# Output projections tile by tile, eight row buffers in the combine, and a rebuilt group norm, in a two-layer encoder with mixture of experts

## The chip, the cores and the metric

One Trainium2 chip; the kernel runs on one of its cores. Its engines work side by side and meet only through semaphores: TensorE (PE) multiplies matrices, VectorE (DVE) and ScalarE (ACT) compute elementwise, GpSimd (POOL) builds masks and issues gathers, SyncE (SP) issues weight loads. The metric is the device time of one execution in microseconds, lower is better.

## The reference

Two batches of 256 tokens of width 1024 (512 token rows in all) go through two layers. Layer 0 mixes with a gated recurrence and a delta-rule recurrence (RWKV-7), layer 1 with windowed attention; behind each stands a mixture of 32 experts, two of them for a token.

```python
def trunk(x):
    for i in range(2):
        h = rms_norm(x, norm_mix[i])
        mix = recurrent_mixer(h, ...) if i == 0 else window_attention(h, ...)
        x = x + mix
        h = rms_norm(x, norm_ffn[i])
        x = x + hier_moe(h, ...)

# end of recurrent_mixer, its last steps: per-head group norm (8 heads of 64), bonus, gate, output projection
y = y_f + y_b
mu = mean(y, -1); var = mean(square(y - mu), -1)
yn = (y - mu) * rsqrt(var + 64e-5) * ln_w + ln_b
bonus = sum(r * (k_f + k_b) * r_k, -1) * v
rw_out = (yn + bonus) * (sigmoid(gd) @ g_up)
return concatenate([rg_out, rw_out]) @ w_out          # (512, 1024) @ (1024, 1024)

def hier_moe(x, wg1, bg1, wg2, bg2, w_gate, w_up, w_down):
    group_prob = softmax(x @ wg1 + bg1)               # 4 groups
    fine = x @ wg2[group] + bg2[group]                # 8 experts of the chosen group
    top_p, top_e = top_k(softmax(fine), 2)
    gate = top_p / sum(top_p) * max(group_prob)
    # tokens sorted by expert, then for each expert:
    hb = silu(xb @ w_gate[e]) * (xb @ w_up[e])        # 1024 -> 512, float32
    out = hb @ w_down[e]                              # 512 -> 1024
    y[token] += out * gate
```

## The kernel before

The 512 token rows are four tiles of 128 (t = 0 to 3), kept in `X` as 128 x 1024 each. All of it is float32; a product of 512 columns on PE is two passes (two MATMUL records). The order of work on each engine is the order in which the program is written; semaphores alone make one engine wait for another.

Recurrence and group norm. After the delta-rule loop its output lies in `yT`, four feature tiles of 128 x 512 (two heads each). The group norm goes through them one at a time: PE sums a head's 64 rows with the block mask `blk` (L1802), the bonus's sums (L1803) and the gate product (L1804); DVE subtracts the mean (L1579), ACT squares (L1348), PE sums again (L1807), ACT takes the root (L1350), DVE inverts it (L1584) and does four more steps (L1585 to L1589). PE's next tile waits for the last of them:

```python
            for ft in range(FT):
                if ft:
                    pe.wait_ge(gn_out, ft)
```

Output projection. `w_out` lies in two ring slots of 2 MB, one for each half h of the 1024 output columns. The loop is `for h: for t:` with eight products of two passes each (L1818 in layer 0, L872 in layer 1) into banks 4 to 7, and DVE adds each result to `X` (L1597, L987). So every tile is complete only in the second half of the loop.

Norm. `act_norm`, `dve_norm`, `pe_turn_norm` and `act_hT` run behind the last add: ACT squares and sums all four tiles (L211), one root (L214), DVE inverts (L218) and scales four tiles into `xn` (L220), PE turns them chunk by chunk (L229; 32 transposes), ACT copies each chunk with the norm's weights (L235). They run four times: before the recurrence (j = 0), before the experts of layer 0 (j = 1), before the attention (j = 2) and before the experts of layer 1 (j = 3).

Router. PE multiplies the turned rows with the router's 36 columns (L537; 32 products), DVE picks group and experts (L404 to L431), PE ranks the tokens within their experts with 14 products of 32 columns (L543 to L547), DVE makes the one-hot dispatch matrix (L449 to L436), PE gathers the rows of the first two experts with it (L559).

Experts. 16 pairs of experts; in each pair PE does gate and up (L578) and down (L587) of both, and the dispatch of the next pair. SP streams the weights (2 MB each, six a pair) into the six ring slots. The first loads wait as the table `FIRST` says, the later ones for a product that frees their slot. ACT stores each expert's rows to `expert_rows` in device memory.

Combine. When all rows are stored, POOL gathers for each token tile the rows of its first expert (k = 0) and of its second (k = 1), eight gathers of 128 rows, into the four buffers of `rows`; a gather into a used buffer waits for the add that reads it. DVE adds them to `X` (L511), first all tiles with k = 0 and then with k = 1. In layer 0 the norm of the attention follows, in layer 1 the stores of the result.

## Time and profile before

| | us |
|---|---|
| time, median of 3 runs | 2159.3 (2156.1 to 2162.61) |
| the profiled execution: its time | 2155.26 |
| the profiled execution: span from first to last instruction | 2153.4 |
| PE busy | 1887.0 (88%) |
| DVE busy | 721.3 (33%) |
| ACT busy | 417.9 (19%) |
| mean granted TensorE clock | 0.926 |

The span is a sequence of stages with different limits: projections and the recurrence's chunk products (to 641 us), the group norm (to 696), output projection, norm and router (to 805), the experts of layer 0 (to 1286), combine and norm (to 1327), attention (to 1530), its output projection, norm and router (to 1642), the experts of layer 1 (to 2125), and the last combine. The shares of busy time in the table are means over all of these, so each stage has to be read by itself. A granted clock of 1.00 is TensorE's level of 2.4 GHz, 0.50 its level of 1.2 GHz.

### The profile page before, as it was taken

The numbers are of one execution on the slowest core, as the hardware profiler recorded it, in microseconds if no ns is written. First come the engines' busy times: TensorE is split into PE (matmuls) and PEld (weight loads), VectorE is DVE, ScalarE is ACT, GpSimd is POOL, SyncE is SP. The second block draws the span as 40 slices with busy tenths as digits, with TensorE's granted clock in tenths as the row PEclk, the third lists the DMA queues.
The fourth block names the chain that finished last, engine by engine and source line by source line (L and its number), as shares of the span: only waits on it lengthen the run. The fifth ranks groups of instructions, "written<-read, shape, count | busy, mean of one in ns | idle before, by whom it ended". The sixth has DMA issues, their size and how long they took to land.

```text
span 2153.4 us, 22208 instructions
## 1 busy us (share of the span) xinstructions
PE 1887.0 (88%) x8696; PEld 990.5 (46%) x8696; DVE 721.3 (33%) x1200; ACT 417.9 (19%) x812; POOL 66.5 (3%) x104
## 2 busy tenths in 40 slices
PE   6997199999984979999999974978988999999993
PEld 3443188888871453333333322467554333333331
DVE  2137966766735132111111103566114111111112
ACT  3116322222220021111111112244121111111110
POOL 3120000000000000000000001000000000000001
PEclk9998599999996969999999997997888999999996
DMA  8000000000001418999999977210013999999996
GB/s 268 0 0 0 0 1 1 0 0 0 0 32 66 176 40 362 429 429 428 429 429 429 428 319 293 78 40 1 8 71 135 427 429 427 430 429 428 429 429 219
DMA packets 68281, 459.72 MB, mean 213 GB/s; under 512 B 18748, under 2 KB 19910, under 8 KB 43654
## 3 DMA queue, kind: packets, MB, share of 16 engines
q1 hardware_dynamic: 55402, 433.77, 48.6%
q10 hardware_dynamic: 10524, 16.86, 2.2%
q0 software_dynamic: 2304, 8.39, 1.2%
q8 instruction: 34, 0.56, 0.1%
q14 instruction: 17, 0.14, 0.0%
HBM read 440.12 MB, written 18.87 MB: 213 GB/s over the span
## 4 chain that ended last, share of the span: by engine, by line
PE 76%; DVE 10%; DMA 6%; ACT 5%; issue 2%; ACTq 0%; POOL 0%; DVEq 0%; SPq 0%; POOLq 0%
PE bank L578 20%; PE bank L559 10%; PE bank L587 9%; PE bank L1624 7%; DMA ring<-in_moe_w_up_dram 4%; PE bank L1736 4%; PE bank L793 3%; PE bank L1744 3%; PE bank L1818 3%; PE bank L872 3%; PE bank L1767 2%; PE bank L1752 1%; PE bank L566 1%; DVE ring L1562 1%; DMA arena<-expert_rows,dest 1%
## 5 line engine op out<-in xcount | busy, mean ns | idle before, releaser
L578 PE MATMUL bank<-ring,arena 128*64 128x512 f32 x2048 | 456.6, 598 | 11.1 <-DMA ring<-in_moe_w_up_dram 8.8
L496 DVE TENSOR_TENSOR arena<-arena,bank 64x512 f32<-64x512 f32 x64 | 67.0, 1046 | 705.3 <-ACT arena L366 705.2
L578 PEld LDWEIGHTS bank<-ring,arena 128*64 128x64 f32 x2048 | 149.4, 138 | 309.3 <-issue 306.8
L559 PE MATMUL bank<-xn,arena 128*128 128x512 f32 x512 | 242.0, 617 | 3.0 <-DVE arena L436 3.0
L587 PE MATMUL bank<-ring,arena 128*64 128x512 f32 x1024 | 228.2, 598 | 1.4 <-ACT arena L376 1.4
L559 PEld LDWEIGHTS bank<-xn,arena 128*128 128x128 f32 x512 | 94.2, 194 | 148.3 <-issue 145.1
L1624 PE MATMUL bank<-hT,ring 128*128 128x512 f32 x336 | 144.5, 592 | 0.8 <-ACT hT L235 0.8
L587 PEld LDWEIGHTS bank<-ring,arena 128*64 128x64 f32 x1024 | 71.0, 137 | 135.9 <-issue 134.0
L366 ACT ACTIVATE arena<-bank 64x512 f32<-64x512 f32 x64 | 37.8, 591 | 424.5 <-PE bank L578 424.5
L1736 PE MATMUL bank<-ring 128*128 128x128 f32 x768 | 100.7, 283 | 5.5 <-DVE ring L1557 4.5
L1624 PEld LDWEIGHTS bank<-hT,ring 128*128 128x128 f32 x336 | 63.8, 190 | 80.9 <-issue 79.9
L1544 DVE TENSOR_TENSOR Zb<-bank,lvlmask 128x512 f32<-128x512 f32 x112 | 76.7, 690 | 67.1 <-PE bank L1736 66.5
L1744 PE MATMUL bank<-ring,Zb 128*128 128x128 f32 x768 | 98.8, 282 | 0.0
L1736 PEld LDWEIGHTS bank<-ring 128*128 128x128 f32 x768 | 90.8, 193 | 13.1 <-DVE ring L1557 7.6
L1744 PEld LDWEIGHTS bank<-ring,Zb 128*128 128x128 f32 x768 | 90.2, 193 | 4.0 <-issue 1.2
L1767 PE MATMUL bank<-ring 64*128 64x256 f32 x256 | 40.6, 418 | 52.8 <-DVE arena L1517 52.8
L381 ACT ACTIVATE arena<-bank 128x512 f32<-128x512 f32 x64 | 38.2, 598 | 228.4 <-PE bank L587 228.4
L361 ACT ACTIVATE arena<-bank 128x512 f32<-128x512 f32 x64 | 38.2, 597 | 217.4 <-PE bank L559 217.4
L443 DVE TENSOR_TENSOR arena<-bank,gffn 128x512 f32<-128x512 f32 x64 | 41.3, 687 | 114.9 <-PE bank L566 114.9
L1562 DVE TENSOR_TENSOR ring<-bank,ring 128x512 f32<-128x512 f32 x96 | 65.7, 691 | 39.0 <-PE bank L1744 37.0
L1326 ACT ACTIVATE ring<-bank 128x512 f32<-128x512 f32 x80 | 47.8, 598 | 150.5 <-PE bank L1752 148.9
L229 PE MATMUL bank<-ident,xn 128*128 128x128 f32 x128 | 29.7, 380 | 52.7 <-DVE xn L220 51.6
(307 smaller groups left out, 1912.1 us busy)
## 6 DMA issues: line engine op xcount, KB each, us to landing
ring<-in_moe_w_gate_dram SPq DMA_DIRECT2D x64, 2048.0 KB, 14.2
ring<-in_moe_w_up_dram SPq DMA_DIRECT2D x64, 2048.0 KB, 18.7
ring<-in_moe_w_down_dram SPq DMA_DIRECT2D x64, 2048.0 KB, 16.3
expert_rows<-arena ACTq DMA_DIRECT2D x128, 128.0 KB, 10.0
ring<-in_rec_w_in_dram SPq DMA_DIRECT2D x5, 2048.0 KB, 13.5
ring<-in_att_w_in_dram SPq DMA_DIRECT2D x3, 2048.0 KB, 9.8
ring<-in_rec_w_out_dram SPq DMA_DIRECT2D x2, 2048.0 KB, 10.3
ring<-in_att_w_out_dram SPq DMA_DIRECT2D x2, 2048.0 KB, 18.8
```

The lines of the kernel that those rows point to most:

```text
L496: nc.vector.tensor_tensor(by_chunk(hb[par * CAP:(par + 1) * CAP, :]), by_row(sg[0:CAP, par, :]), by_row(bank[par][CAP:2 * CAP, :]), ALU.mu ...
L559: mm = nc.tensor.matmul(bank[2 + h][:, :], onehot[:, t, :, :].rearrange("p k s -> p (k s)"), xn[:, t, h * 512:(h + 1) * 512], start=(t == ...
L578: mm = nc.tensor.matmul(bank[par][k * CAP:(k + 1) * CAP, :], xg[:, c, par * CAP:(par + 1) * CAP], W[k][:, c * FF:(c + 1) * FF], start=(c = ...
L587: mm = nc.tensor.matmul(bank[6 + par][h * CAP:(h + 1) * CAP, :], hT2[:, f, par * CAP:(par + 1) * CAP], W[:, f * D + h * 512:f * D + (h + 1 ...
L793: mm = nc.tensor.matmul(bank[2 + i % 4][:, :], W[:, c, (i % 4) * P:(i % 4 + 1) * P], hT[:, c, :], start=(c == 0), stop=(c == KC - 1))
L872: mm = nc.tensor.matmul(bank[4 + i % 4][:, :], hT[:, c, t * P:(t + 1) * P], W[:, c, :], start=(c == 0), stop=(c == KC - 1))
L1544: nc.vector.tensor_tensor(Zb[:, 4 * q:4 * q + 4, :], m4(bank[q][:, :]), four(lvlmask[:, d, l, :]), ALU.mult).then_inc(z_out, 1)
L1562: ins = nc.vector.tensor_tensor(dst, m4(bank[2 + q][:, :]), dst, ALU.add)
L1624: mm = nc.tensor.matmul(o, W[:, c, (f % 4) * P:(f % 4 + 1) * P], hT[:, c, :], start=(c == 0), stop=(c == KC - 1))
L1736: mm = nc.tensor.matmul(o, M[:, p, 0, :], Tt[:, p, 0, :], start=True, stop=True)
L1744: mm = nc.tensor.matmul(bank[2 + q][:, i * P:(i + 1) * P], Zb[:, p, :], Tt[:, p, 1, :], start=True, stop=True)
L1767: mm = nc.tensor.matmul(bank[p % 6][:, k * 256:(k + 1) * 256], BKt[d][hs, k, c, :], ARt[d][hs, c, :, :].rearrange("p a t -> p (a t)"), sta ...
```

## The change

Six edits, all in the order of work and its helpers; the products of projections, recurrence, attention and experts stay.

1. Output projections go tile by tile (`for t: for h:`). Between them PE turns the tile before and multiplies it with the router; ACT squares, DVE scales and weighs a tile while PE projects the next one. Four of a tile's eight turned chunks are weighed by DVE (one instruction), four by ACT (four instructions). The turned tiles lie in a ring of two (`hTt`); the normed rows of layer 0 lie in `hT` since `xn` is still read.
2. The other two norms (j = 0 and 2) go tile by tile as well.
3. The combine has eight row buffers, the four new ones where the experts' buffers were; a tile's two gathers count on one semaphore, and in layer 0 the norm of a tile stands between the adds of the next.
4. The group norm handles its four tiles side by side: the mean is subtracted by PE with a centring matrix, variances of all eight heads are summed into 8 rows, one root and one inverse of 8 x 512 serve all tiles, and PE spreads the inverse back over the heads. POOL builds the masks for it.
5. The ranks come from 5 products of 160 to 32 columns instead of 14 of 32; one memset is added on DVE.
6. Smaller: the tables of DVE and the bias row are made before the projection; the two down loads of the first pair wait for the seventh and eighth projection (before: fourth and eighth); the semaphores of the overflow blocks are merged.

```diff
+        def act_rms(act, j, t):
+            ...
+            nc.scalar.activation(XN[j][:, t, :], X[:, t, :], ACT.Square, accum_out=ssq[:, t:t + 1]).then_inc(ssq_ready, 1)
+            act.wait_ge(ssq_ready, TT * j + t + 1)
+            nc.scalar.activation(rstd[:, t:t + 1], ssq[:, t:t + 1], ACT.Sqrt, scale=1.0 / D, bias=eps_rms).then_inc(rms_ready, 1)
+        def pe_turn(pe, j, t):
+            pe.wait_ge(xn_ready, TT * j + t + 1)
+            if t:
+                pe.wait_ge(hT_dve, TT * j + t)
+                pe.wait_ge(hT_act, TT * j + t)
+            for half in range(2):
+                for c in range(4):
+                    mm = nc.tensor.transpose(bank[half][:, c * P:(c + 1) * P],
+                                             XN[j][:, t, (4 * half + c) * P:(4 * half + c + 1) * P], ident[:, :])
+                mm.then_inc(hT_raw, 1)
+        def act_turned(act, j, t):
+            act.wait_ge(hT_raw, 2 * (TT * j + t) + 2)
+            ...
+            for c in range(4):
+                ins = nc.scalar.activation(turned(j, t)[:, 4 + c, :], bank[1][:, c * P:(c + 1) * P], ACT.Copy, scale=VA[:, col:col + 1])
+        def pe_project_out(pe, l, done, project):
+            j = 2 * l + 1
+            for t in range(TT):
+                for h in range(2):
+                    i = 2 * t + h
+                    if i >= 4:
+                        pe.wait_ge(x_updated, 16 * l + i - 3)
+                    project(t, h, bank[4 + i % 4][:, :]).then_inc(done, 1)
+                    if t and h == 0:
+                        pe_turn(pe, j, t - 1)
+                    elif t:
+                        route_logits(pe, l, t - 1)
+            pe_turn(pe, j, TT - 1)
+            route_logits(pe, l, TT - 1)
+        def dve_project_out(dve, step, l, done):
+            for t in range(TT):
+                for h in range(2):
+                    ...
+                    nc.vector.tensor_tensor(x, x, bank[4 + i % 4][:, :], ALU.add).then_inc(x_updated, 1)
+                    if t and h == 0:
+                        dve_turned(dve, j, t - 1)
+                dve_scale(dve, step, j, t)
+            dve_turned(dve, j, TT - 1)
...
-            for k in range(2):
-                for t in range(TT):
-                    i = k * TT + t
-                    dve.wait_ge(rows_loaded[i % 4], 16 * (2 * l + i // 4 + 1))
...
+            for t in range(TT):
+                dve.wait_ge(rows_loaded[t], 32 * (l + 1))
+                add_rows(t, 0)
+                if t and not last:
+                    dve_scale(dve, step, 2, t - 1)
+                dve.wait_ge(x_updated, 8 + 16 * l + 2 * t + 1)
+                add_rows(t, 1)
+                if t and not last:
+                    dve_turned(dve, 2, t - 1)
...
+            nc.tensor.matmul(bank[3][:, 0:(TT + 1) * EXPERTS], chunkmask[:, 0, 0, :], flat_e, start=True, stop=False)
+            for b in range(1, TT + 1):
+                mm = nc.tensor.matmul(bank[3][:, b * EXPERTS:(TT + 1) * EXPERTS], ones[:, :],
+                                      flat_e[:, 0:(TT + 1 - b) * EXPERTS], start=False, stop=(b == TT))
...
-        FIRST = ([[(gn_out, FT)], [], [], [], [(out_done, 4)], [(out_done, 8)]],
+        FIRST = ([[(gn_out, FT)], [], [], [], [(out_done, 7)], [(out_done, 8)]],
...
             for ft in range(FT):
-                if ft:
-                    pe.wait_ge(gn_out, ft)
-                nc.tensor.matmul(bank[0][:, :], blk[:, :], yT[:, ft, :], start=True, stop=True).then_inc(gn_mean, 1)
+                nc.tensor.matmul(bank[ft][:, :], centre, yT[:, ft, :], start=True, stop=True).then_inc(gn_mean, 1)
+            for ft in range(3):
+                bonus(ft)
+            for ft in range(FT):
                 pe.wait_ge(gn_sq, ft + 1)
-                nc.tensor.matmul(bank[1][:, :], blk[:, :], e2[:, 0:T], start=True, stop=True).then_inc(gn_var, 1)
+                mm = nc.tensor.matmul(bank[4][0:8, :], head_sum[:, ft, :], gn_y2[:, ft, :], start=(ft == 0), stop=(ft == 3))
+            mm.then_inc(gn_var, 1)
+            pe.wait_ge(gn_sqrt, 1)
+            bonus(3)
+            pe.wait_ge(gn_rs, 1)
+            for ft in range(FT):
+                pe.wait_ge(gn_bonus, ft + 1)
+                nc.tensor.matmul(bank[gn_bank[ft]][:, :], head_of[:, ft, :], gn_r8[0:8, 1, :],
+                                 start=True, stop=True).then_inc(gn_bc, 1)
+            for ft in range(FT):
+                pe.wait_ge(gn_scaled, ft + 1)
+                nc.tensor.matmul(bank[ft][:, :], LUP[64:128, 0, ft * P:(ft + 1) * P], wag[64:128, :],
+                                 start=True, stop=True).then_inc(gn_gate, 1)
```

On PE, from the last round of the group norm in layer 0 to the ranks, before:

```order
L1802 MATMUL bank<-xn,blk 128x512
L1803 MATMUL bank<-arena,blk 128x512
L1804 MATMUL bank<-arena 128x512
L1807 MATMUL bank<-ring,blk 128x512
L1818 MATMUL bank<-ring,xn 128x512 x64
L1048 MATMUL bank<-brow,ones 128x88
L229 MATMUL bank<-ident,xn 128x128 x32
L537 MATMUL bank<-wr,hT 128x36 x32
L543 MATMUL bank<-arena,chunkmask 128x32 x2
```

And now, from the start of the group norm into the second tile's projection:

```order
L1888 MATMUL bank<-xn,lvlmask 128x512 x4
L1891 MATMUL bank<-arena,blk 128x512 x3
L1896 MATMUL bank<-ring,lvlmask 8x512 x4
L1891 MATMUL bank<-arena,blk 128x512
L1903 MATMUL bank<-ring,lvlmask 128x512 x4
L1907 MATMUL bank<-arena 128x512 x4
L1912 MATMUL bank<-brow,ones 128x88
L1922 MATMUL bank<-ring,xn 128x512 x24
L240 MATMUL bank<-ident,hT 128x128 x8
L1922 MATMUL bank<-ring,xn 128x512 x8
L303 MATMUL bank<-wr,arena 128x36 x8
L1922 MATMUL bank<-ring,xn 128x512 x8
```

The rounds of the group norm are drawn into one, and the transposes (L240) and the router's products (L303) of a tile stand between the projections (L1922) of the next.

On DVE, one feature tile of the group norm before (xn is where `yT` lies, ring is scratch):

```order
L1579 SCALAR_TENSOR_TENSOR xn<-bank,xn 128x512
L1582 TENSOR_TENSOR ring<-bank,arena 128x512
L1584 RECIPROCAL ring<-ring 128x512
L1585 TENSOR_TENSOR xn<-xn,ring 128x512
L1586 TENSOR_SCALAR xn<-xn,VA 128x512
L1588 TENSOR_TENSOR xn<-xn,ring 128x512
L1589 TENSOR_TENSOR xn<-xn,bank 128x512
```

And now the first twelve rows for all four tiles:

```order
L1663 TENSOR_TENSOR ring<-bank,arena 128x512 x3
L1665 RECIPROCAL ring<-ring 8x512
L1667 TENSOR_TENSOR ring<-bank,arena 128x512
L1671 TENSOR_TENSOR xn<-ring,bank 128x512 x2
L1675 SCALAR_TENSOR_TENSOR xn<-xn,VA,ring 128x512
L1671 TENSOR_TENSOR xn<-ring,bank 128x512
L1675 SCALAR_TENSOR_TENSOR xn<-xn,VA,ring 128x512
L1681 TENSOR_TENSOR xn<-xn,bank 128x512
L1671 TENSOR_TENSOR xn<-ring,bank 128x512
L1675 SCALAR_TENSOR_TENSOR xn<-xn,VA,ring 128x512
L1681 TENSOR_TENSOR xn<-xn,bank 128x512
L1675 SCALAR_TENSOR_TENSOR xn<-xn,VA,ring 128x512
```

Seven steps a tile have become four, and four inversions have become one.

On DVE, the combine of layer 0 and the norm behind it (arena holds the gathered rows), before:

```order
L688 MEMSET small 128x1
L511 SCALAR_TENSOR_TENSOR X<-arena,X 128x1024 x8
L218 RECIPROCAL rstd<-rstd 128x4
L220 TENSOR_SCALAR xn<-X,rstd 128x1024 x4
L926 CAST arena<-lvlmask 128x256
```

And now:

```order
L771 MEMSET small 128x1
L596 SCALAR_TENSOR_TENSOR X<-arena,X 128x1024 x3
L230 RECIPROCAL rstd<-rstd 128x1
L231 TENSOR_SCALAR xn<-X,rstd 128x1024
L596 SCALAR_TENSOR_TENSOR X<-arena,X 128x1024
L252 TENSOR_TENSOR hT<-bank,VA 128x4x128
L596 SCALAR_TENSOR_TENSOR X<-arena,X 128x1024
```

The inversion, the scaling and DVE's share of the turned tile have moved in among the adds.

## Rows read from the trace of the kernel before

**Rows 1.** The page's first line: the span.
```profile
span 2153.4 us, 22208 instructions
```
**Rows 2.** Busy us (xinstructions) by stretch: PE PEld DVE ACT POOL, PEclk, DMA share, GB/s.
```profile
735.00:753.00 18.00, 17.85 (x42) 7.60 (x40) 1.49 (x3) 0.00 (x0) 0.00 (x0) 1.00 0.00 0
812.60:1285.60 473.00, 462.24 (x1928) 171.48 (x1928) 63.02 (x83) 63.29 (x110) 0.00 (x0) 1.00 0.98 416
```
**Rows 3.** Timeline, group norm: start, us, engine, line, operation, idle before and releaser.
```profile
641.21 2.07 PE L1802 MATMUL bank<-xn,blk 128*128 128x512 f32 x2 [1.29 <-POOL xn L1152]
...
647.19 0.69 ACT L1350 ACTIVATE ring<-bank,small 128x512 f32<-128x512 f32 x1 [1.14 <-PE bank L1807]
647.98 3.35 DVE L1584 RECIPROCAL ring<-ring 128x512 f32<-128x512 f32 x1 [1.15 <-ACT ring L1350]
...
695.68 57.17 PE L1818 MATMUL bank<-ring,xn 128*128 128x512 f32 x128 [6.99 <-DVE xn L1589]
```
**Rows 4.** Stretches, PE alone: busy (xpasses), PEclk, DMA share, GB/s.
```profile
645.00:649.00 4.00, 2.15 (x4) 0.99 1.04 395
695.60:699.60 4.00, 3.92 (x5) 0.50 0.76 238
```
**Rows 5.** Timeline, behind layer 0's output projection; last, layer 1's first routing step.
```profile
752.88 0.69 DVE L1597 TENSOR_TENSOR X<-X,bank 128x512 f32<-128x512 f32 x1 [6.18 <-PE bank L1818]
...
758.45 2.74 DVE L220 TENSOR_SCALAR xn<-X,rstd 128x1024 f32<-128x1024 f32 x4
...
768.11 10.94 PE L537 MATMUL bank<-wr,hT 128*128 128x36 f32 x64 [0.78 <-ACT hT L235]
779.09 0.31 DVE L404 TENSOR_TENSOR arena<-bank,bb 128x144 f32<-128x144 f32 x1 [17.90 <-PE bank L537]
...
1616.20 0.31 DVE L404 TENSOR_TENSOR arena<-bank,bb 128x144 f32<-128x144 f32 x1 [20.33 <-PE bank L537]
```
**Rows 6.** The chain that ended last: layer 1's output projection (start us, us, what).
```profile
1529.63 56.64 PE bank L872 x128
```
**Rows 7.** Stretches of norm and router in layer 0, PE alone.
```profile
759.00:764.00 5.00, 4.16 (x15) 0.50 0.12 49
764.00:768.00 4.00, 3.03 (x19) 0.93 0.02 4
768.00:770.00 2.00, 1.89 (x17) 1.00 0.00 0
```
**Rows 8.** Timeline, ranks in layer 0: first products, and the step behind the last.
```profile
784.83 1.06 PE L543 MATMUL bank<-arena,chunkmask 128*128 128x32 f32 x4 [5.77 <-DVE arena L422]
...
791.11 0.29 DVE L449 SCALAR_TENSOR_TENSOR arena<-bank,arena 128x128 f32<-128x128 f32 x1 [4.98 <-PE bank L547]
```
**Rows 9.** Timeline, combine and norm of layer 0, start of attention.
```profile
1298.11 5.27 DVE L511 SCALAR_TENSOR_TENSOR X<-arena,X 128x1024 f32<-128x1024 f32 x4 [20.48 <-DMA arena<-expert_rows,dest]
...
1311.38 1.06 ACT L211 ACTIVATE xn<-X 128x1024 f32<-128x1024 f32 x1 [25.20 <-DVE X L511]
...
1315.66 1.28 ACT L214 ACT_TABLE_LOAD   x1
...
1327.33 14.00 PE L793 MATMUL bank<-hT,ring 128*128 128x512 f32 x32 [0.78 <-ACT hT L235]
```
**Rows 10.** Timeline, last combine: the second of its gathers and its last add.
```profile
2130.84 0.94 POOL L525 DMA_INDIRECT arena<-expert_rows,dest  x1 [0.30 <-issue]
...
2149.07 1.28 DVE L511 SCALAR_TENSOR_TENSOR X<-arena,X 128x1024 f32<-128x1024 f32 x1 [1.40 <-DMA arena<-expert_rows,dest]
```
**Rows 11.** The page's gathers: count, median us from issue to landing.
```profile
arena<-expert_rows,dest POOLq DMA_INDIRECT x16, 5.5
```
**Rows 12.** Timeline, last pairs of layer 0: eight transposes; a gate and up.
```profile
1247.60 1.09 PE L566 MATMUL bank<-ident,arena 128*128 128x128 f32 x8 [0.25 <-ACT arena L361]
...
1266.92 8.45 PE L578 MATMUL bank<-ring,arena 128*64 128x512 f32 x32 [3.79 <-DMA ring<-in_moe_w_up_dram]
```
**Rows 13.** Groups by line and form: busy us, mean ns of one, idle before.
```profile
L1302 ACT ACTIVATE arena<-bank,arena 64x64 f32<-64x64 f32 x32 | 9.9, 310 | 25.7 <-PE bank L1713 25.4
```

More of the change, by code:

```diff
@@ L314, in trunk @@
         over = [dict((n, sem(f"over_{n}{l}")) for n in (
-            "loaded", "onehot", "xg_raw", "xg", "gu", "sg", "hb", "turned", "hT", "down", "ob",
-            "sum", "added", "step")) for l in range(2)]
+            "loaded", "dve_built", "pe_built", "act_copied", "down", "sum", "added")) for l in range(2)]
         over_end = sem("over_end")
```

336 lines of the change are left out of this document (183 added, 153 removed).

## The prediction, made before the changed kernel was run

> **What bounds the kernel now.** Two times go into the sum: the profiled execution took 2155.3 us, 1.9 more than its span [rows 1]. I read the stretches stage by stage first, then the chain that ended last, then the timeline wherever PE stood still.
>
> The experts are bound by their weight stream: DMA is busy 0.98 of that stage and the clock is full [rows 2], and at its end PE waits 3.8 us for a weight block [rows 12]. Nothing in the change touches that stage's work. But its stream starts only when the first gate and up free a slot: before that DMA is idle, 0.00 even during the projection [rows 2]. So the stage is a block of fixed length, and whatever brings its first gate and up forward moves its end by the same amount. What can be won lies in the stretches between such blocks, where PE waits for chains of DVE and ACT: the group norm (641.2 to 695.7, [rows 3]), norm and router (to 779.1 in layer 0 and 1616.2 in layer 1, [rows 5]), ranks [rows 8], combine and norm [rows 9], last combine [rows 10].
>
> **Group norm.** Before, four rounds of about 13.6 us one behind the other: 695.68 - 641.21 = 54.5 [rows 3]. Now one chain, in times of the old trace. The unit prices: a pass of 512 columns on PE is 0.855 us at the 1.2 GHz level (a pair of them is seen by its reader after about 2.2) and 0.43 at the other, by 57.17 us for 128; a DVE or ACT step of 128 x 512 is 0.7, the inverse of 512 columns 3.35 [rows 3]. The eight rows of the new inverse don't make it shorter; I take the price by columns.
> - PE: four centrings, three bonus sums and four head sums are 22 passes from 641.2. Before, the clock was full from 645 on [rows 4]; with 5 passes slow and 17 fast they end at 652.8. The squares (four of 0.7, a pass or two behind PE) hide beside the bonus sums. Sum seen 653.1.
> - Root 0.75 (its table load stands behind the squares, hidden), inverse 3.4: 657.3. First spread 1.1, first ACT copy 0.75: 659.2.
> - Then DVE is the bound: 12 steps (scale, add, gate for each tile) of 0.73 = 8.8, to 668.1, and 0.4 to the projection: 668.5.
> - PE waits about 2.5 us for the inverse. If its clock falls there, the spreads and gates cost 1 to 3 us more. I take 670.0.
> Gain 25.7. Bounds: everything at 1.2 GHz gives 679.3, a gain of 16.4; no loss at all and a projection that starts warm (its first five passes took 3.92 instead of 2.15, [rows 4]) gives 29. POOL's masks are 13 small instructions that no row shows; they run while POOL waits for the last chunk's outputs, which it adds before the first centring (its releaser, [rows 3]). Were they late, that centring would wait by at most their own length.
>
> **Projection, norm and router.** Before, layer 0: 695.68 to 779.09 = 83.4, of which 57.2 is projection, 10.9 the router and the rest waiting [rows 3, 5]. Layer 1: 1529.63 to 1616.20 = 86.6 [rows 5, 6]. Now PE does in this stretch the 57.2, and inside it three blocks of eight transposes (1.09 as a whole, [rows 12]; I take 1.0) and two router blocks of 16 passes. The router ran 17 passes in 2 us at full clock [rows 7], so 2.0 each: 57.2 + 3.0 + 4.0 = 64.2 at the end of the last projection. Each transposes' wait is covered: the chain add, square, root, scale is about 3.6 us and the projection that stands between is 6.9 (an eighth of 55).
>
> Behind the last projection a chain remains for one tile: add 0.74; square to scale 1.7 (before: 758.45 - 753.57 = 4.9 with four squares, less three at 1.06, [rows 5, 9]); scale 0.69; eight transposes 1.09; ACT's four copies; 16 router passes 2.0 to 2.9; semaphores 0.4. The third tile's router block lies beside add, square and scale. A copy of 128 x 128 with a scale is not in the trace: 0.31 for 64 columns is the nearest row [rows 13], 0.69, an ACT step of 512 columns, the other end [rows 3]; I take 0.33, near the first, four are 1.3. With 2.8 for the router the chain is 9.0. So 73.2 against 83.4: gain 10.2 in layer 0. In layer 1, 56.6 + 7.0 + 9.0 = 72.6 against 86.6: gain 13.9 (there the root's table load and a slower router go too).
>
> The two down loads start up to 30 us later than before. DMA is idle then [rows 2], they need some 10 us, and the first down comes more than 30 us behind them: no cost.
>
> **Ranks.** 28 passes took 784.83 to 791.11 = 6.3, or 0.22 each at a slow clock [rows 8]. Now 10 passes, of which the widest has 160 columns (0.27 by the price of 512): 2.8 with the wait of the reader. The memset on DVE's chain costs 0.15. Gain 3.4 in each layer, 6.8.
>
> **Combine and norm in layer 0.** Before, DVE's first add stands at 1298.11, the last ends at 1311.35 and the attention's first product at 1327.33 [rows 9]. The four adds from 1298.11 ran on end, so two gathers had landed by 1299.4, and with eight buffers the other six are issued at intervals of 1.24 (0.94 + 0.30, [rows 10]) without waiting for an add. Now each tile takes two adds (1.32 each), inverse and scale 0.9 and DVE's turned half 0.72: 4.2 us. From 1299.0 the first tile is added at 1301.6; square and table load 1.28 [rows 9] delay its scale to 1304.7; the further tiles are added at 1307.0, 1311.2 and 1315.5. Behind that: 1.7 + 0.69 + 1.09 + 1.3 + 0.3 = 5.1, so 1320.6, a gain of 6.7. Before, 29 transposes in a row came right in front and the projection began warm (14.00 for 32 passes); now they come eight at a time, so I charge half of a cold start, 1.1: gain 5.6, from 2 to 8.
>
> **Last combine.** The eighth gather is issued at 2130.84 + 6 x 1.24 = 2138.3, up to 2 later if DVE's adds slow POOL; it lands 5.5 later [rows 11], at 2143.8 to 2146; two adds follow: 2146.5 to 2148.7, against 2150.35 [rows 10]. I take a gain of 2.1; between -1 and 4.
>
> **First norm.** ACT's chain grows (four copies a tile instead of eight large ones) and its overlap grows; I come out at equality, with 1.5 either way.
>
> **Sum.** 25.7 + 10.2 + 13.9 + 6.8 + 5.6 + 2.1 = 64.3. From 2155.3 that is 2091.0; the median of the runs stands 4.0 above the profiled execution, so 2095.0.
>
> **The rivals.**
> - The clock falls in the interleaved projections. The router's narrow products and the waits between could let it fall at each of the six inserts a layer; each fall costs a warm-up like the one at 695.6, five passes, 2.1 us [rows 4]. 12 x 2.1 = 25: 2120. For it: a router block is 2 us of little work. Against it: transposes alone brought the clock from 0.50 to 0.93 [rows 7], and the experts keep 1.00 with such transposes in every pair [rows 2, 12].
>  The Trainium skill (TensorE: Matmul & The Clock Gate, Part 4: PE-mode transpose) states that transposes don't count as a busy PE and don't bring up the full clock; by that rule the inserts would be idle to the clock and this rival the likelier outcome, 2120. The trace disagrees here: nothing but transposes ran on PE as the clock rose, and by that row the sum stays. Chance 13%.
> - The stream of weights doesn't follow: were the experts' end fixed by something other than the first freed slot, all gains ahead of the two expert stages were waited off and only the last combine's stayed. 2157, no change. For it: DMA is the bound at the end of the stage [rows 12]. Against it: DMA idles before the stage begins [rows 2]. Chance 2%.
> - The tiles don't overlap as written, a wait holding each transposes block until the router's turn: then only group norm, ranks and last combine gain, 34.6: 2125. For it: ACT's queue holds roots and copies in turn. Against it: 3.6 of chain under 6.9 of cover. Chance 4%.
> - Slower: the projections run at the 1.2 GHz level throughout, because small inserts every 7 us keep it from rising. 16 projections of 13.7 instead of 6.9 are +110; net +46, 2205. It decides from 59% of the passes at that level (64.3 of 110). After 695.6 the level rose within five passes of sixteen [rows 4], which speaks against it. Chance 3%.
>
> **How the numbers follow.** The forecast holds 78%: its own range, by the bounds of group norm (16 to 29), the two projection stretches (15 to 27), ranks (5 to 8) and combines (1 to 12), taken as unlikely to lie at one end together, is 2082 to 2111. The range reaches 2080 to 2114, with part of the first rival. A measurement here can't tell less than 0.3% (6 us) from no change. Faster: forecast, the first and third rival and half a percent for mixtures, 0.95; same 0.02; slower 0.03.
>
> **What would show it.** Right: projection of layer 0 starting near 670; the first routing step 73 us behind it in both layers; first gate and up near 764 instead of 805; the expert stages of unchanged length (about 480); attention beginning 5 to 6 us sooner behind the last experts' store; one inverse of 3.35 us over 8 rows. Wrong: a granted clock under 0.9 during the projections, DVE's scales waiting longer than 7 us, or an expert stage that grows by what was won ahead of it.

## The result and the profile after

The changed kernel takes 2098.4 us (median of 4 runs, 2091.6 to 2107.5), the kernel before 2159.7 (4 runs, 2156.1 to 2162.6): ratio 0.9715, 95% interval 0.9691 to 0.9738, 61.3 us less. Forecast: 2095, 2080 to 2114. A later set of five runs gave 2098.6 and a ratio of 0.9716 (0.9692 to 0.9739). The profiled execution took 2091.61 with a span of 2089.9; that of the later set (run 10, called "again" here) has a span of 2100.8, and the two, which ran the same program, show how far a single stage may be trusted.

Lengths of the stages in us, from the first start of one line to the first start of the next (starts read to 0.1), with the gain against before in brackets:

| stage | before | forecast gain | after | after, again |
|---|---|---|---|---|
| start to group norm | 641.2 | 0 | 647.3 (-6.1) | 646.9 (-5.7) |
| group norm | 54.5 | 25.7 | 30.0 (24.5) | 32.6 (21.9) |
| projection, norm, router, layer 0 | 83.4 | 10.2 | 72.9 (10.5) | 72.7 (10.7) |
| routing and dispatch, layer 0 | 26.4 | 3.4 | 21.5 (4.9) | 21.4 (5.0) |
| experts 0, first gate and up to last down | 479.4 | 0 | 478.1 (1.3) | 481.5 (-2.1) |
| combine and norm | 42.4 | 5.6 | 35.9 (6.5) | 35.5 (6.9) |
| attention, up to its output projection | 202.3 | 0 | 205.0 (-2.7) | 206.0 (-3.7) |
| projection, norm, router, layer 1 | 86.6 | 13.9 | 72.4 (14.2) | 74.6 (12.0) |
| routing and dispatch, layer 1 | 26.0 | 3.4 | 21.2 (4.8) | 21.5 (4.5) |
| experts 1 | 482.4 | 0 | 477.8 (4.6) | 480.3 (2.1) |
| last combine | 28.8 | 2.1 | 27.8 (1.0) | 27.8 (1.0) |
| sum | | 64.3 | 63.5 | 52.6 |

The windows of the changed kernel (width, busy time and count of each engine, granted clock, DMA's share, GB/s), to be laid beside [rows 2, 4, 7]:

```profile
core 0: us, PE busy (x) PEld busy (x) DVE busy (x) ACT busy (x) POOL busy (x), PEclk, DMA share, GB/s
677.31:750.20 72.89, 69.96 (x225) 37.37 (x224) 12.58 (x27) 11.63 (x29) 0.00 (x0) 0.94 0.44 173
701.00:746.00 45.00, 42.67 (x154) 23.09 (x152) 8.74 (x16) 8.48 (x24) 0.00 (x0) 1.00 0.22 79
771.70:1250.40 478.70, 468.07 (x1960) 173.63 (x1960) 69.54 (x102) 63.27 (x109) 0.00 (x0) 1.00 0.97 411
1490.70:1563.10 72.40, 69.44 (x224) 37.21 (x224) 11.69 (x21) 12.92 (x30) 0.00 (x0) 0.95 0.16 58
```

PE is now busy 70 of 73 us between the first pass of the projection and the first routing step, and the clock stays at 1.00 from 701 to 746, across all inserts that lie there (second row). The experts' stage is the same block, 34 us earlier.

The timeline of the changed kernel in the group norm (start, duration, engine, line, tile, idle time before and its releaser), against [rows 3]:

```profile
647.32 5.50 PE L1888 MATMUL bank<-xn,lvlmask 128*128 128x512 f32 x8 [1.29 <-POOL xn L1218]
658.96 0.68 ACT L1427 ACTIVATE ring<-bank,small 8x512 f32<-8x512 f32 x1 [4.21 <-PE bank L1896]
659.67 3.34 DVE L1665 RECIPROCAL ring<-ring 8x512 f32<-8x512 f32 x1 [3.55 <-ACT ring L1427]
663.07 5.69 PE L1903 MATMUL bank<-ring,lvlmask 8*128 8x512 f32 x8 [2.25 <-DVE ring L1665]
668.68 7.19 PE L1907 MATMUL bank<-arena 64*128 64x512 f32 x8
675.91 0.69 DVE L1681 TENSOR_TENSOR xn<-xn,bank 128x512 f32<-128x512 f32 x1 [1.02 <-PE bank L1907]
...
677.31 7.15 PE L1922 MATMUL bank<-ring,xn 128*128 128x512 f32 x11
```

One chain instead of four, with one inverse over eight rows that is as long as one over 128 (3.34). Behind it DVE waits for PE (last gate, 1.02): the granted clock fell to the low level during the spreads (0.64 as a mean of 663.0 to 668.7) and was 0.50 in the gates.

A seam between tiles and the end of the stage, same view, against [rows 5]:

```profile
700.17 1.04 PE L240 MATMUL bank<-ident,hT 128*128 128x128 f32 x8
701.05 7.03 PE L1922 MATMUL bank<-ring,xn 128*128 128x512 f32 x16
701.25 1.14 ACT L261 ACTIVATE arena<-bank,VA 128x128 f32<-128x128 f32 x4 [5.54 <-PE bank L240]
707.92 1.87 PE L303 MATMUL bank<-wr,arena 128*128 128x36 f32 x16
708.12 0.69 DVE L314 TENSOR_TENSOR X<-X,bank 128x512 f32<-128x512 f32 x1 [6.46 <-PE bank L1922]
710.55 0.75 DVE L231 TENSOR_SCALAR hT<-X,rstd 128x1024 f32<-128x1024 f32 x1
716.57 1.04 PE L240 MATMUL bank<-ident,hT 128*128 128x128 f32 x8
...
744.14 1.09 PE L240 MATMUL bank<-ident,hT 128*128 128x128 f32 x8 [1.56 <-DVE hT L231]
746.56 3.60 PE L303 MATMUL bank<-wr,arena 128*128 128x36 f32 x16 [1.32 <-ACT arena L261]
750.20 0.31 DVE L489 TENSOR_TENSOR arena<-bank,bb 128x144 f32<-128x144 f32 x1 [4.67 <-PE bank L303]
```

At 700, 708 and 716 PE has no idle time before transposes and router: the second tile's scale is done at 711.3, its transposes come at 716.6. Only the last tile's transposes and router wait (1.56, 1.32), and that router takes 3.60 instead of 1.87.

Combine and norm, and the last combine, against [rows 9, 10]:

```profile
1264.25 0.94 POOL L620 DMA_INDIRECT arena<-expert_rows,dest  x1 [0.30 <-issue]
1278.52 1.28 DVE L596 SCALAR_TENSOR_TENSOR X<-arena,X 128x1024 f32<-128x1024 f32 x1
1282.49 1.94 PE L240 MATMUL bank<-ident,xn 128*128 128x128 f32 x8 [1.85 <-ACT hT L261]
1285.70 15.74 PE L875 MATMUL bank<-hT,ring 128*128 128x512 f32 x32 [1.28 <-issue]
...
2084.22 2.61 DVE L596 SCALAR_TENSOR_TENSOR X<-arena,X 128x1024 f32<-128x1024 f32 x2 [1.72 <-DMA arena<-expert_rows,dest]
```

All gathers are issued by 1265.2, DVE's last add ends at 1279.8. The attention's first 32 passes take 15.74, before 14.00.

### The profile page after: what moved, and what is told of

Read it like the earlier page. It is cut to its first block, busy times and chain, and to the rows that moved or that the text cites. A ratio compares the mean times of both kernels' runs of the same rounds, so it can differ in the third digit from the quotient of the medians.

```text
span 2089.9 us, 22236 instructions
## 1 busy us (share of the span) xinstructions
PE 1863.5 (89%) x8668; PEld 978.4 (47%) x8668; DVE 718.6 (34%) x1219; ACT 419.6 (20%) x857; POOL 67.3 (3%) x117
## 4 chain that ended last, share of the span: by engine, by line
PE 77%; DVE 9%; DMA 7%; ACT 4%; issue 2%; ACTq 0%; POOL 0%; DVEq 0%; SPq 0%; POOLq 0%
PE bank L661 20%; PE bank L642 10%; PE bank L670 9%; PE bank L1711 7%; DMA ring<-in_moe_w_up_dram 5%; PE bank L1823 4%; PE bank L875 3%; PE bank L1831 3%; PE bank L1922 3%; PE bank L953 3%; PE bank L1839 1%; PE bank L1854 1%; PE bank L649 1%; DVE ring L1647 1%; PE bank L940 1%
## 5 line engine op out<-in xcount | busy, mean ns | idle before, releaser
L661 PE MATMUL bank<-ring,arena 128*64 128x512 f32 x2048 | 452.3, 594 | 10.8 <-DMA ring<-in_moe_w_up_dram 8.4
L661 PEld LDWEIGHTS bank<-ring,arena 128*64 128x64 f32 x2048 | 148.0, 137 | 306.1 <-issue 303.6
L1711 PE MATMUL bank<-hT,ring 128*128 128x512 f32 x336 | 147.0, 600 | 1.3 <-issue 1.3
L642 PE MATMUL bank<-hT,arena 128*128 128x512 f32 x256 | 119.9, 612 | 1.5 <-DVE arena L522 1.5
L642 PE MATMUL bank<-xn,arena 128*128 128x512 f32 x256 | 119.7, 611 | 1.5 <-DVE arena L522 1.5
L1823 PEld LDWEIGHTS bank<-ring 128*128 128x128 f32 x768 | 91.7, 194 | 12.8 <-DVE ring L1642 7.3
L642 PEld LDWEIGHTS bank<-hT,arena 128*128 128x128 f32 x256 | 46.7, 192 | 73.5 <-issue 71.9
L642 PEld LDWEIGHTS bank<-xn,arena 128*128 128x128 f32 x256 | 46.7, 192 | 73.2 <-issue 71.6
```

Source lines behind the costliest of these rows:

```text
L642: mm = nc.tensor.matmul(bank[2 + h][:, :], onehot[:, t, :, :].rearrange("p k s -> p (k s)"), XN[2 * l + 1][:, t, h * 512:(h + 1) * 512], s ...
L661: mm = nc.tensor.matmul(bank[par][k * CAP:(k + 1) * CAP, :], xg[:, c, par * CAP:(par + 1) * CAP], W[k][:, c * FF:(c + 1) * FF], start=(c = ...
L1711: mm = nc.tensor.matmul(o, W[:, c, (f % 4) * P:(f % 4 + 1) * P], hT[:, c, :], start=(c == 0), stop=(c == KC - 1))
L1823: mm = nc.tensor.matmul(o, M[:, p, 0, :], Tt[:, p, 0, :], start=True, stop=True)
```

## The experiments

Runs 1 to 6 are the changed kernel with one edit each, runs 7 to 9 with several, run 10 without any. Times are medians; stage lengths come from one profiled execution and are counted as in the table above. The kernel before, run beside each set, took 2158.1 to 2160.1.

**1. The group norm of before.**

```diff
-                nc.tensor.matmul(bank[ft][:, :], centre, yT[:, ft, :], start=True, stop=True).then_inc(gn_mean, 1)
...
+                if ft:
+                    pe.wait_ge(gn_out, ft)
+                nc.tensor.matmul(bank[0][:, :], blk[:, :], yT[:, ft, :], start=True, stop=True).then_inc(gn_mean, 1)
...
```

> The changed kernel with the group norm of before (four rounds one behind the other); all else as in the changed kernel. Theory A (expert stages are blocks of fixed length that follow their first gate and up): the group norm takes 54.5 us again instead of 30.0, everything behind it moves by these 24.5 us, the expert stage of layer 0 stays at 479 us, and the median goes from 2098.4 to about 2123 (2119 to 2127). Rival B (the weight stream sets the experts' end by itself): the expert stage shrinks by what is lost ahead of it, and the time stays near 2098.

Measured: 2123.0 (2122.8 to 2123.7). The group norm took 57.1, the expert stage of layer 0 481.4. The end moved by 24.6, where the group norm alone is 24.5 (against the second profile of the changed kernel, 32.6) to 27.1 us longer (against the first, 30.0): what is lost ahead of an expert stage is lost at the end, and the expert stage doesn't shrink. Rival B falls, and with it the prediction's second rival.

**2. The old order of the projections.**

```diff
-            for t in range(TT):
-                for h in range(2):
-                    i = 2 * t + h
+            for h in range(2):
+                for t in range(TT):
+                    i = h * TT + t
...
-                    if t and h == 0:
-                        pe_turn(pe, j, t - 1)
-                    elif t:
-                        route_logits(pe, l, t - 1)
+            for t in range(TT - 1):
+                pe_turn(pe, j, t)
+                route_logits(pe, l, t)
```

> The changed kernel with only the order of the two output projections as before (all tiles of the first half of the columns, then all of the second); norm, transposes and router stay tile by tile but now all lie behind the projection. Theory A (what is won there is the cover: three tiles' chains lie under the projection): behind the projection stand four rounds of transposes, copies and router of about 5 us each instead of one chain of 9, so each layer's stretch from the first pass to the first routing step grows by 7 to 13 us (72.9 to 80-86), and the time to 2112-2124. Rival B (the gain comes from the norm by tiles alone, one square and one root at a time, and not from the order): each stretch stays within 2 us of 73 and the time within 2098 +- 5.

Measured: 2121.1 (2115.4 to 2123.8); the stretches took 83.0 and 82.9. The timeline behind the projection of layer 0, and its window:

```profile
734.40 1.04 PE L240 MATMUL bank<-ident,hT 128*128 128x128 f32 x8
737.97 2.30 PE L303 MATMUL bank<-wr,arena 128*128 128x36 f32 x16 [2.54 <-ACT arena L261]
740.08 1.95 PE L240 MATMUL bank<-ident,hT 128*128 128x128 f32 x8
743.35 3.60 PE L303 MATMUL bank<-wr,arena 128*128 128x36 f32 x16 [1.32 <-ACT arena L261]
```

```profile
734.00:760.40 26.40, 19.81 (x98) 18.05 (x96) 5.06 (x10) 7.19 (x20) 0.00 (x0) 0.60 0.23 84
```

The norm by tiles alone gains next to nothing against before (83.0 and 83.4): all of the 10 us in layer 0 lies in the order, and 10.5 of layer 1's 14.2 (82.9, before 86.6). Behind the projection each router block waits for ACT, and from the second tile on transposes and router take about twice as long (1.95 and 3.60; the granted clock of the whole window is 0.60); under the projection they cost 1.04 and 1.87. A is what happened.

**3. Four row buffers.**

```diff
-        row_buf = [rows[:, b, :] for b in range(4)] + [AR[:, row2 + b * D:row2 + (b + 1) * D] for b in range(4)]
+        row_buf = [rows[:, b % 4, :] for b in range(8)]
...
+                    if 2 * t + k >= 4:
+                        pool.wait_ge(x_updated, 8 + 16 * l + 2 * t + k - 3)
```

> The changed kernel with four row buffers in the combine instead of eight: from the fifth gather on each waits for an add. Order of tiles and norm by tiles stay. Theory A (the buffers matter in both layers): the gathers of tiles 2 and 3 wait for the adds of tiles 0 and 1; in layer 0 DVE's adds are themselves held up by the norm's steps between them, so combine and norm grow by 3 to 7 us from 35.2, the last combine by 1 to 3 from 27.2; time 2103 to 2108. Rival B (the gain of layer 0 lies in the norm by tiles, the buffers only run ahead of a chain that is longer anyway): less than 1 us in each, time 2098 to 2100.

Measured: 2104.0 (2099.9 to 2106.5). Combine and norm 36.6 (0.7 more than 35.9; the expectation counts both stages from 0.6 us later), last combine 32.0 (4.2 more, from 28.8 in the kernel before). Its last combine:

```profile
2081.76 1.86 POOL L622 DMA_INDIRECT arena<-expert_rows,dest  x1 [3.37 <-DVE X L596]
2092.04 2.60 DVE L596 SCALAR_TENSOR_TENSOR X<-arena,X 128x1024 f32<-128x1024 f32 x2 [5.74 <-DMA arena<-expert_rows,dest]
```

Neither theory: B holds in layer 0, where the norm's steps fill DVE between the adds (the 0.7 lies within the spread of this stage: with eight buffers it took 34.6 to 37.5 in the other profiles whose combine is that of the changed kernel), and in layer 1 the loss is larger than A said. With two gathers to a tile the fifth waits for the first add and DVE then waits 5.74 us. So the order by tiles alone makes the last combine 3.2 us worse than before, and the eight buffers pay that back and 1.0 more.

**4. The 14 rank products.**

```diff
-            nc.tensor.matmul(bank[3][:, 0:(TT + 1) * EXPERTS], chunkmask[:, 0, 0, :], flat_e, start=True, stop=False)
...
+            for t in range(TT):
+                o = bank[3][:, t * EXPERTS:(t + 1) * EXPERTS]
+                mm = nc.tensor.matmul(o, chunkmask[:, 0, 0, :], Eany[:, t, :], start=True, stop=(t == 0))
```

> The changed kernel with the 14 rank products of before (28 passes) instead of 5 (10 passes). The stretch from the first routing step to the first gate and up became 4.9 us shorter in layer 0 and 4.7 in layer 1, where 3.4 was forecast. Theory A (all of it is the products: 3.9 us of PE and a shorter wait of the reader): the stretch grows back by 4 to 5 us in each layer, time about 2107. Rival B (the products give only the 3.4, and the rest is PE's clock in the dispatch behind them): the products cost 3.4 and the dispatch of 8.9 us stays as it is; time about 2105, the stretch grows by 3 to 3.6.

Measured: 2108.2 (2107.9 to 2108.7); the stretch 25.3 and 25.1, 3.8 and 3.9 more, the dispatch 8.94 as with the new products (8.90). Between the two: the products give 3.8 to 3.9, about A's size. The other 1.1 and 0.9 of the gain in this stretch lie where B looked for them, in the dispatch behind the ranks: in the kernel before it took 10.18 in layer 0 and 9.76 in layer 1, here 8.94 and 8.79, at a mean granted clock of 0.79 in layer 0 against 0.69 before. What brought the clock up sooner there no run shows. The time grew by 9.8, the two stretches by 7.7; the rest stands in stages that this edit doesn't touch.

**5. No cover.**

```diff
-                    if t and h == 0:
-                        pe_turn(pe, j, t - 1)
-                    elif t:
-                        route_logits(pe, l, t - 1)
+                pe_turn(pe, j, t)
+                route_logits(pe, l, t)
```

> The changed kernel, but each tile's transposes and router come directly behind that tile's own two projections, not one tile later; so PE waits for add, square, root, scale and for the copies of every tile. Theory A (the gain of order is cover: 3.6 us of chain before the transposes and 1.4 before the router, hidden under the next tile's projection): three more tiles a layer are exposed with about 5 us each, the stretch from first pass to first routing step grows from 72.9 and 72.4 to 87 to 89, time 2125 to 2132. Rival B (the same, and PE's clock falls in each of these waits, a warm-up of 2 us each): 93 to 95 a layer, time 2138 to 2145, and the granted clock of these stretches is under 0.85. Rival C (waits are covered otherwise): within 3 us, time 2098 to 2105.

Measured: 2159.8 (2156.3 to 2165.0, 10 runs), ratio to before 1.000 (0.999 to 1.002). The stretch of layer 0 took 100.9, and its windows show why (the whole, then from the first and from the second router on), with PE behind the first tile in the timeline:

```profile
677.50:778.40 100.90, 82.47 (x225) 44.79 (x224) 12.81 (x26) 11.63 (x29) 0.00 (x0) 0.82 0.32 125
698.00:706.00 8.00, 6.90 (x21) 5.02 (x22) 0.07 (x1) 0.95 (x4) 0.00 (x0) 0.57 0.02 8
722.00:732.00 10.00, 8.68 (x25) 5.60 (x23) 0.53 (x1) 1.14 (x4) 0.00 (x0) 0.52 0.00 0
```

```profile
696.68 1.09 PE L240 MATMUL bank<-ident,hT 128*128 128x128 f32 x8 [3.27 <-DVE hT L231]
699.10 3.60 PE L299 MATMUL bank<-wr,arena 128*128 128x36 f32 x16 [1.33 <-ACT arena L261]
702.50 15.37 PE L1916 MATMUL bank<-ring,xn 128*128 128x512 f32 x32
```

B is right in kind and too small. Each tile's waits cost PE 3.3 and 1.3 us, and router and first passes of the next projection then run at the 1.2 GHz level: the router takes 3.60 instead of 1.87, a tile's 32 projection passes 15.4 to 16.8 instead of 13.8 (32 at 0.43). In layer 0 that makes 28.0 us, some 15 of them waits and the rest slower passes; in layer 1 the stretch took 105.7, 33.3 more. Together they are the whole loss of 61.4. The prediction's first rival is a real mechanism; the cover keeps it away. Tiles in the right loop order but one step too early would have made this whole change worth nothing.

**6. The first norm of before.**

```diff
-            pe_turn_all(pe, 0)
+            for c in range(KC):
+                if c >= 2:
+                    pe.wait_ge(hT_first, c - 1)
+                for t in range(TT):
+                    if c == 0:
+                        pe.wait_ge(xn_ready, t + 1)
+                    mm = nc.tensor.transpose(bank[c % 2][:, t * P:(t + 1) * P], xn[:, t, c * P:(c + 1) * P], ident[:, :])
...
```

> The changed kernel with the first norm of before (all squares, one root, 32 transposes chunk by chunk); the other three norms by tiles. The first projection began 1.5 us later than in the kernel before and ran 2.5 us longer (w_in's products 147.0 us instead of 144.5). Theory A (eight transposes at a time between waits leave the clock low, 21 in a row bring it up): first projection at 26.6 again, its products 144.5, the group norm's start 4 us sooner than 647.3 (but for what the recurrence itself varies), time about 2094. Rival B (chance: such a start varies by itself from kernel to kernel): products stay at 146 to 147, only the 1.5 us come back, time 2097.

Measured: 2094.3 (2088.2 to 2105.1); first projection at 26.3. The group of w_in's products, from the page of this run and of the changed kernel (busy us, mean ns | idle before):

```profile
L1730 PE MATMUL bank<-hT,ring 128*128 128x512 f32 x336 | 144.5, 592 | 0.8 <-ACT hT L279 0.8
```

```profile
L1711 PE MATMUL bank<-hT,ring 128*128 128x512 f32 x336 | 147.0, 600 | 1.3 <-issue 1.3
```

A's numbers, in the profile: 4.3 us at the end of this stage come back. That is not chance: these products took 144.4 to 144.5 us in the five profiles with the norm of before or that of runs 7 to 9, and 145.8 to 147.0 in all seven with the norm by tiles. A's reason, the clock, is read from the length of the passes alone: the first 8 took 6.20 us in the changed kernel, the first 18 took 7.99 in the kernel before, but the granted clock reads 1.00 there in both (20 to 36 us). And the edit changes ACT's work and the order of the transposes together. The medians (2094.3 and 2098.4) don't tell it apart, since the recurrence behind it took 473.9 here and 468.0 to 473.9 in all runs, with nothing changed in it.

**7. PE kept at work with products, and a quicker first norm.** The products' results are not read; all else is computed.

```diff
+        def warm(b, n, kind="product"):
+            for _ in range(n):
+                if kind == "product":
+                    nc.tensor.matmul(bank[b][:, :], ident[:, :],
+                                     chunkmask[:, 0, :, :].rearrange("p a b -> p (a b)"), start=True, stop=True)
+                else:
+                    for c in range(4):
+                        nc.tensor.transpose(bank[b][:, c * P:(c + 1) * P], chunkmask[:, 0, c, :], ident[:, :])
...
+            warm(4, 1, "product")
             pe_turn(pe, j, TT - 1)
+            warm(4, 1, "product")
             route_logits(pe, l, TT - 1)
+            warm(4, 6, "product")
...
```

> The changed kernel with (1) the first norm's squares and roots all first on ACT and two pairs of banks for its transposes, and (2) PE kept at work in waits: products of constants whose result nobody reads, in the first norm's end (8 transposes), in the group norm's wait for the inverse (4 passes) and behind its last two gates (2 each), before and behind the last tile's transposes (2 each), behind the last router (12), behind the ranks (2), and in the attention's norm (4 before, 4 behind each of three tiles, 2 behind the last). Theory A (what is left on PE in these places runs at 1.2 GHz because PE stood still before it): first projection at about 23, its products 144.5; group norm 27 instead of 30.0; the last router 1.9 instead of 3.6, the dispatch 6.9 instead of 8.9 in both layers, the attention's first 32 passes 14.0 instead of 15.7; time 2074 to 2082. Rival B (the clock follows something else than such work, or the waits of DVE and ACT set these stretches): only the first norm's 4 to 5 us come, 2093; the unread products may cost up to 1 us at each place, 2100 at worst.

Measured: 2084.5 (2082.8 to 2086.2). Router 1.95, dispatch 7.13 in layer 0, attention's first passes 13.97, first projection at 23.3 and its products 144.4: A, but for the group norm, 33.4 instead of 27, because the products behind the third gate held the fourth (DVE waited 3.32 us for it). That puts the time 2.5 above A's range.

**8. The same with transposes.** Against run 7, here behind the last projection:

```diff
-            warm(4, 1, "product")
+            warm(4, 2, "turn")
             pe_turn(pe, j, TT - 1)
-            warm(4, 1, "product")
+            warm(4, 2, "turn")
             route_logits(pe, l, TT - 1)
-            warm(4, 6, "product")
+            warm(4, 9, "turn")
...
```

> As the run before, with transposes of constants in place of the products in all of these places (four of 128 x 128 for each, somewhat more of them, since a product of 512 columns takes 0.86 us and four transposes 0.52). Theory A (transposes hold the clock as products do, as the rise from 0.50 to 0.93 under transposes in the kernel before says): within 4 us of the run with products, the last router 1.9, the dispatch 6.9. Rival B (by the Trainium skill, TensorE: Matmul & The Clock Gate, Part 4: PE-mode transpose, transposes are no work to the clock): the places stay at 1.2 GHz, router 3.6, dispatch 8.9, attention's first products 15.7; time 12 to 18 us above the run with products.

Measured: 2080.5 (2074.8 to 2081.6). Its timeline (L297 are the added transposes, L321 the last router, L661 the dispatch, L899 the attention's first products):

```profile
738.54 1.95 PE L321 MATMUL bank<-wr,arena 128*128 128x36 f32 x16 [0.45 <-ACT arena L264]
740.31 4.13 PE L297 MATMUL bank<-ident,chunkmask 128*128 128x128 f32 x36
749.26 7.13 PE L661 MATMUL bank<-hT,arena 128*128 128x512 f32 x16 [0.58 <-DVE arena L540]
...
1273.27 13.97 PE L899 MATMUL bank<-hT,ring 128*128 128x512 f32 x32 [0.40 <-issue]
```

Rival B falls in each of its places: 1.95 for 3.60, 7.13 for 8.90, 13.97 for 15.74, as with products (and 1.95 and 7.13 again in layer 1). In this kernel the rule of the Trainium skill (TensorE: Matmul & The Clock Gate, Part 4: PE-mode transpose) doesn't hold; the prediction was right to go by [rows 7].

**9. The group norm rearranged.** As 8, with the first two gates in the wait for the inverse:

```diff
+        spread_bank, gate_bank = [7, 4, 7, 4], [5, 6, 0, 1]
...
+            gate(0)
+            gate(1)
             pe.wait_ge(gn_rs, 1)
...
+            for ft in range(2, FT):
+                pe.wait_ge(gn_scaled, ft - 1)
+                gate(ft)
+            pe.wait_ge(gn_sq, FT + 3)
+            warm(7, 5, "turn")
```

> The run with transposes in the waits (first norm, last router, ranks, attention's norm), with the group norm rearranged instead of filled: the gate products of tiles 0 and 1 stand in the wait for the inverse, the spreads use two banks in turn, the gates of tiles 2 and 3 follow, and behind them 20 transposes of constants. In the changed kernel PE was the bound behind the inverse: 16 passes of 8 and 64 rows at 0.855 us are 13.7 us from 663.1. Theory A (with four of these passes moved into the wait DVE's 12 steps of 0.73 set the end again): the group norm takes 26 to 28 us instead of 30.0 to 32.7 and the projection starts at full clock; time 2072 to 2078. Rival B (passes of 64 rows bring the clock down themselves, so that the spreads run at 0.855 each): 28 to 30 us, time 2077 to 2082.

Measured: 2078.5 (2071.4 to 2084.9), ratio to before 0.962 (0.959 to 0.965). The group norm took 29.0. Its timeline (L1931 gates, L1942 spreads, L1706 DVE's last two gate steps, L298 transposes):

```profile
650.28 1.98 PE L1931 MATMUL bank<-arena 64*128 64x512 f32 x4
652.60 5.67 PE L1942 MATMUL bank<-ring,lvlmask 8*128 8x512 f32 x8 [0.34 <-DVE ring L1690]
...
661.71 1.28 DVE L1706 TENSOR_TENSOR xn<-xn,bank 128x512 f32<-128x512 f32 x2
661.91 3.62 PE L298 MATMUL bank<-ident,chunkmask 128*128 128x128 f32 x20
```

By its numbers the run lies in B's ranges, group norm and time, and just outside A's. A's chain is there (DVE was done 26.2 us after the first centring, and the projection began at 1.00), but the added transposes ran 2.5 us beyond it. B's sign is there in part: the spreads took 5.67, 0.71 a pass, at a clock of 0.64. So the run doesn't decide between them. Against run 8 the median shows no difference (2078.5 and 2080.5); both are 18 to 20 us faster than the changed kernel (2098.4 and 2098.6, about 1%), and these two are the best versions found.

**10. The changed kernel again.**

> The changed kernel once more, beside the run before on the same chip. Theory A: 2098 +- 4; the recurrence's stretch from the products behind w_in to the group norm, whose code is the same in all kernels here and took between 468.0 and 473.9 us in eight of them, lies in these bounds again, as do the expert stages (478 to 483). Rival B: the lengths that this kernel showed (472.4, 478.1, 477.8) are its own and come back to 0.3 us.

Measured: 2098.6; recurrence 472.6, expert stages 481.5 and 480.3. A: the expert stages don't come back to 0.3. The second profile of the same program differs by 10.9 us, most of it in the group norm (2.6), experts (3.4 and 2.5), attention and its projection (3.2). Windows of the group norm, of this run and then of the first, from its start and behind the inverse (in the first run the gates too):

```profile
646.90:652.60 5.70, 5.67 (x7) 2.50 (x8) 0.00 (x0) 1.34 (x3) 0.00 (x0) 0.50 0.95 354
663.00:668.00 5.00, 4.24 (x5) 1.82 (x6) 1.94 (x3) 1.11 (x2) 0.00 (x0) 0.50 0.00 0
```

```profile
647.30:652.60 5.30, 5.28 (x8) 2.30 (x9) 0.00 (x0) 1.79 (x3) 0.00 (x0) 0.65 0.97 355
663.00:668.70 5.70, 5.63 (x9) 1.86 (x9) 3.49 (x7) 2.06 (x3) 0.00 (x0) 0.64 0.00 0
668.70:677.30 8.60, 7.82 (x11) 2.98 (x10) 5.13 (x9) 0.69 (x1) 0.44 (x2) 0.50 0.00 0
```

The clock rose and fell at other points of the same work; that is the 2.6 us (the centrings 1.1 longer, the spreads 1.5).

## Why the prediction was right, and where its terms were off

- **Group norm (25.7).** The chain was the one written down: root at 659.0 where the forecast, moved by the later start, says 659.2, inverse 3.34. Behind it the forecast had DVE as the bound and took 1.5 us for a clock that falls in the wait. It fell, in the second profile in that wait (0.50 from 663.0, the first spread at 663.8), in the first only within the spreads (1.00 until 664, 0.50 from 665, the first spread at 663.1), and PE became the bound, not DVE: 16 passes of spreads and gates took 12.8 us in one run (663.1 to 675.9) and 14.3 (7.19 and 7.19) in the other. Gain 24.5 and 21.9; the four other runs with this group norm whose other edits lie behind it show 30.0 once and 32.5 to 32.6 three times. Against experiment 1 and the second run, 57.1 and 32.6, the gain is again 24.5. Within the bounds, the term 1 to 4 too high.
- **Projection, norm and router (10.2 and 13.9).** Measured 10.5 and 14.2 (12.0 in the second run). Inserts cost 1.04 and 1.87 as priced, the last tile's chain ended 9.3 us behind the last projection (740.9 to 750.2; forecast 9.0). There is some luck in that: the forecast's parts add up to 8.7, and the last router took 3.60 where 2.8 was taken. Experiment 2 shows that it is the order, experiment 5 that it is the cover.
- **Ranks (3.4 a layer).** 4.9 and 4.8 in the stretch, of them 3.8 and 3.9 by experiment 4; from the first new product to the step that reads the last it took 2.5 us (756.1 to 758.6) where 2.8 was forecast. The rest is a shorter dispatch, which the forecast didn't have.
- **Combine (5.6).** 6.5 and 6.9. But the eight buffers, which the forecast took as what lets the gathers run ahead, are not what wins it (0.7 in experiment 3, inside the spread of this stage); what is left of the change here is the adds by tiles with the norm among them, which no run undid by itself. And half a cold start was charged (1.1) where more came, 1.7, in the attention's first products; with it the measured term is 4.8.
- **First norm (0 +- 1.5).** This step failed. The first projection began 1.5 later, and its products took 2.5 longer (2.0 and 1.4 in the second profile); experiment 6 ties both to the norm by tiles. That the transposes come eight at a time between waits and leave PE slow is the likely reason, not a shown one. The forecast charged that very effect to the attention's norm and left it out here.
- **Last combine (2.1).** 1.0: the last two gathers' issues took 1.23 and 1.01 beside DVE's adds, and DVE had the last rows 7.1 us behind their end (2077.1 to 2084.2). The forecast took 5.5 from issue to landing, the median of the kernel before; in the changed kernel that median is 6.8.
- **Expert stages unchanged.** Yes: 477.7 to 483.3 in all profiles, wherever they began. The 1.3 and 4.6 that the layers seemed to win in the first profile are within this spread. The attention's 2.7 is 1.7 of cold start, and the rest within a spread of its own (202.3 to 212.3).

The sum of 64.3 was met by the medians (61.3), and the mechanism of its largest terms is the one written down. That it came so close is partly luck, with errors on both sides: 6 us lost ahead of the group norm, 1 in the group norm, 1 in the last combine and 2.7 in the attention, against some 3 more won in ranks and dispatch, 1 in the combine, and in the first profile 5.9 in the expert stages, which the change doesn't touch. Without these 5.9 its 63.5 would be 57.6; the second profile has 52.6.

Of the rivals, the falling clock at the inserts didn't come, and no wait stands in front of the inserts under the projection; experiment 5 shows that it is what happens without the cover. It lost 61 us to waits and clock together, as much as the change had won. The third, tiles that don't overlap, falls with the seam shown above, where PE has no idle time at 700, 708 and 716. The fourth, projections at the low level throughout, didn't come either: 1.00 from 701 to 746.

## What to carry to other kernels

Work that waits for a chain of other engines is cheapest one step late: put it behind the next piece of PE's work, so that the chain lies under it. In experiment 5 an idle PE paid twice, 15 us in the waits of layer 0 and 13 in the slower passes behind them; where no useful work could be moved into the wait, unread transposes did as well as products (2080.5 and 2084.5). A gain ahead of a stage of fixed length arrives whole at the end, but single profiles of one program differ by up to 3.4 us a stage here, so judge terms of that size by an undoing experiment and medians.

## What was not expected

- Transposes hold the clock: in run 8, with 36 of them behind the last router (4.13 us, where PE waited 5.93 for the ranks in the changed kernel) and 8 behind the ranks, the dispatch took 7.13 instead of 8.90.
- In run 8 the spreads of 8 rows ran at 1.00 behind 16 transposes, in run 9 at 0.64 behind 4 gate passes of 64 rows, with waits of 0.50 and 0.34 in front; in the two profiles of the changed kernel and in runs 7 to 9 the gates behind the spreads ran at 0.50 to 0.61 though PE hardly stood still. Whether it is the kind of pass that lets the clock fall is open: no run separates it. The recurrence's 32 passes of 32 rows lean that way: in the changed kernel the first 16 (from 192.8) ran at 1.00 and the last 12 (200.6 to 208.0) at 0.50, with PE busy for 7.33 of these 7.4 us and waits of 0.73 and 0.64 us in between, while passes of 128 rows right before them kept 1.00 behind a wait of 0.42.

```profile
656.28:659.90 3.62, 3.62 (x8) 1.40 (x8) 2.06 (x4) 2.06 (x3) 0.00 (x0) 1.00 0.02 5
```

```profile
652.60:658.20 5.60, 5.60 (x8) 1.76 (x8) 3.40 (x6) 2.06 (x3) 0.00 (x0) 0.64 0.00 0
```

The first row is of run 8, the second of run 9: both show PE busy throughout, with eight passes of the same work, 2 us apart.

- From the products behind w_in to the group norm, with the same work on PE, it took 468.0 to 473.9 us in twelve profiles.
